# Expert stages of a two-layer diffusion backbone: ScalarE splits a tile ahead of weighing a gathered pick, and layer two's last V chunk moves to the U tiles' PSUM bank

## The reference, cut to what matters

```python
def peer(h, w_q, sub_keys, u_tab, v_tab):
    experts, gates = peer_route(hf, w_q, sub_keys)     # 8 heads x 16 picks of 16384 experts, per token
    def block(args):
        hb, eb, gb = args
        a = jnp.einsum('td,tkd->tk', hb, u_tab[eb])
        w = gb.astype(hb.dtype) * jax.nn.gelu(a, approximate=False)
        return jnp.einsum('tk,tkd->td', w, v_tab[eb])
...
    x = x + mod[5] * peer(modulate(rmsnorm(x, ln2_w[layer]), mod[3], mod[4]),
                          p_w_q[layer], p_sub_keys[layer], p_u[layer], p_v[layer])
```

## Time and profile before

| what | value |
|---|---|
| median of 3 runs | 4219.02 us (4217.18 to 4225.48) |
| profiled execution, span | 4219.0 us |
| its own time beside the span | 4219.0 us on the same clock: nothing lies around the span |
| PE busy | 3869.5 us (92%) |
| DVE busy | 3528.4 us (84%) |
| ACT busy | 1945.1 us (46%) |
| POOL busy | 1105.8 us (26%) |
| mean HBM traffic | 241 GB/s over the span |
| Gelus of layer one (L1939), first to last start | 1078.3 to 2396.7 us |
| Gelus of layer two (L1939), first to last start | 3236.0 to 4184.3 us |

### The profile page before, as it was taken

How to read it: one execution, slowest core, us unless ns; L and a number is a source line. 1 busy time by engine, 2 the same in 40 slices (tenths; PEclk the granted TensorE clock), 3 DMA queues, 4 the chain that set the end, 5 groups by cost and what they waited for, 6 DMA issues and landing times. The chain is left out here.

```text
span 4219.0 us, 69815 instructions
## 1 busy us (share of the span) xinstructions
PE 3869.5 (92%) x23631; PEld 3337.2 (79%) x23631; DVE 3528.4 (84%) x6910; ACT 1945.1 (46%) x3599; POOL 1105.8 (26%) x1095
## 2 busy tenths in 40 slices
PE   7969989988999999999999897898868999999998
PEld 6854468877888888888888776336767999999998
DVE  5387948999799999999999966666998899999998
ACT  4367532147444444444444355654246444444443
POOL 0000000039443434434334300000046333333332
PEclk9979999869999999999999998999979999999999
DMA  5102321246899999999999821112237999999997
GB/s 194 55 17 65 89 67 46 70 123 191 326 382 364 381 364 381 370 372 370 384 366 383 333 66 46 44 45 77 68 100 247 371 369 376 369 376 369 377 368 290
DMA packets 246997, 1018.18 MB, mean 241 GB/s; under 512 B 17121, under 2 KB 115521, under 8 KB 146641
## 3 DMA queue, kind: packets, MB, share of 16 engines
q0 software_dynamic: 85296, 599.59, 36.7%
q1 hardware_dynamic: 161504, 416.31, 28.2%
HBM read 963.34 MB, written 52.43 MB: 241 GB/s over the span
## 5 line engine op out<-in xcount | busy, mean ns | idle before, releaser
L1397 POOL DMA_INDIRECT rows<-rows,pick_i x512 | 790.6, 1544 | 1156.5 <-DVE y_tok L2663 653.2
L525 PE MATMUL psA<-h_hi,split_hi 128*128 128x448 f32 (+3 forms) x2768 | 971.8, 351 | 88.8 <-DVE xT L2642 54.7
L2027 DVE TENSOR_TENSOR split_lo<-raw,split_hi 128x1024 fp32r<-128x1024 f32 x596 | 727.9, 1221 | 303.2 <-ACT split_hi L1441 296.8
L525 PE MATMUL psA<-h_lo,split_hi 128*128 128x448 f32 (+3 forms) x2768 | 952.1, 344 | 0.0
L525 PE MATMUL psA<-h_hi,split_lo 128*128 128x448 f32 (+3 forms) x2768 | 951.8, 344 | 0.0
L1441 ACT ACTIVATE split_hi<-raw 128x1024 fp32r<-128x1024 f32 x596 | 628.3, 1054 | 304.2 <-DMA raw<-expert_pairs 153.4
L525 PEld LDWEIGHTS psA<-h_hi,split_hi 128*128 128x128 f32 x2768 | 527.5, 191 | 165.6 <-issue 112.8
L2651 DVE CUSTOM_DVE_ANT_1 rows<-rows,h_wide 128x1024 f32<-128x1024 f32 x512 | 624.8, 1220 | 25.5 <-DMA rows<-rows,pick_i 23.4
L2663 DVE SCALAR_TENSOR_TENSOR y_tok<-rows,pick_w,y_tok 128x1024 f32<-128x1024 f32 x444 | 569.1, 1282 | 5.9
L525 PEld LDWEIGHTS psA<-h_hi,split_lo 128*128 128x128 f32 x2768 | 527.3, 190 | 35.6
L525 PEld LDWEIGHTS psA<-h_lo,split_hi 128*128 128x128 f32 x2768 | 527.9, 191 | 33.3
(11 more groups left out here) (344 smaller groups left out, 6321.3 us busy)
## 6 DMA issues: line engine op xcount, KB each, us to landing
raw<-expert_pairs SPq DMA_DIRECT2D x256, 1024.0 KB, 7.2
gates<-g_buf SPq DMA_DIRECT2D x22, 2048.0 KB, 8.7
raw<-tiles SPq DMA_DIRECT2D x84, 512.0 KB, 3.7
raw<-mod_tiles SPq DMA_DIRECT2D x80, 512.0 KB, 3.6
g_in<-gates POOLq DMA_DIRECT2D x32, 896.0 KB, 9.0
g_in<-gates POOLq DMA_DIRECT2D x32, 640.0 KB, 5.9
mod_w<-mod_pairs SPq DMA_DIRECT2D x8, 1024.0 KB, 19.9
rows<-rows,pick_i POOLq DMA_INDIRECT x512, 8.4
```

Source lines behind the costliest of these rows:

```text
L525: ins = nc.tensor.matmul(out_, lhsT, rhs, start=start, stop=stop)
L1397: nc.gpsimd.indirect_dma_start(rows[l][:, b, :], None, (rows0, rows1)[l], bass.IndirectOffsetOnAxis(pick_i[:, u:u + 1], 0))\
L2027: V.tensor_tensor(split_lo[:, n % SPLIT].rearrange("p k n -> p (k n)"), raw[:, n % RAW, :], split_hi[:, n % SPLIT].rearrange("p k n -> p ( ...
```

## The change

Two edits. ScalarE's order around the second Gelu becomes Gelu of u1, split base+2, weigh (before: Gelu, weigh, split); the picks weighed per superblock and their order stay. And layer two's eighth V chunk is treated as layer one's: no longer two resident pieces, but one chunk of 320 columns formed in `psA[0]` after the second Gelu and added to `xT` by VectorE once per superblock. With `CYCLED[1]` no longer None, these lines of before run in layer two as well: TensorE waits for `cycled_free` ahead of u0, `tile_passed` of v0 is given after the cycled chunk instead of after v0's own chunks, VectorE waits for `cycled_full` and adds.

```diff
-RESIDENT = (tuple((k, 0, DENSE[0][1], k, 0) for k in range(KD - 1)),
-            tuple((k, 0, DENSE[1][1], k, 0) for k in range(KD - 1)) +
-            ((KD - 1, 0, 192, 0, 320), (KD - 1, 192, 320, 1, 320)))
-CYCLED = (KD - 1, None)
+RESIDENT = tuple(tuple((k, 0, DENSE[l][1], k, 0) for k in range(KD - 1)) for l in range(DEPTH))
+CYCLED = (KD - 1, KD - 1)
 DRAIN = ((0, 2, 4), (1, 3), (5, 6))
@@ scalar engine, experts(l)
                 for c in range(2):
                     if s + 1 < NSUPER:
                         gelu(c, s + 1)
-                    weigh(spread[2 * c])
+                    if c == 0:
+                        weigh(spread[0])
                     split_to(min(base + c + 1, end))
-                    weigh(spread[1] if c == 0 else 0)
+                    weigh(spread[1 + c])
```

## The result

The changed kernel takes 4110.4 us (median of 4, 4106.6 to 4111.6) against 4218.4 us before: ratio 0.974, 95% interval 0.972 to 0.975. It is faster, by 108 us.

The account below looks back on a forecast made before the run. VectorE's loop, with its idle behind ScalarE's split, was taken to set the pace of both expert stages. 4219.0 less 44 (layer one) less 38 (layer two) gave 4137, stated as 4138 us; range 4115 to 4182.

Parts of the forecast that it names:

- ScalarE's order, VectorE's idle: Both layers: splitting before weighing removes VectorE's whole idle, 1.08 us per superblock in layer one and 1.21 in layer two.
- What is late next in layer one: Layer one: TensorE and VectorE become level at about 19.7 us per superblock, gaining at most 58 us.
- The transfers of layer one: Layer one: 7.80 MB per superblock at 391 GB/s gives a 19.95 us floor; superblock taken as 19.9, gain 44 us.
- Layer two: Layer two: cycled chunk and new order bring the superblock from 14.98 to 14.35 us, within 14.2 to 14.5; gain 38 us.
- (d): Layer two: ScalarE's existing wait for the U pair's transfer costs nothing yet; its window grows by 0.5 us.
- (a): Layer two: TensorE's next U tile must wait for VectorE's add, a short wait of 0.1 to 0.2 us per superblock.
- (b): Layer two: the cycled chunk must wait for the second Gelu, which is done two us before.
- (c): Layer two: first V tile's slot returns only after the cycled chunk; ScalarE's split still fits with 0.1 us to spare.
- the transfers as bound: Rival: transfers bound layer one, superblock 20.25 us, gain 24; layer two at 14.5 gains 29; 4166 us; chance 0.19.
- the ring's late slot: Rival: returned slot or add late by 0.8 us keeps layer two at 14.98 us; 4175 us in all; chance 0.13.
- the slower one: Rival: TensorE waits over 1.5 us for layer two's add; at 16.0 us a superblock, 4237 us; chance 0.05.
- the order that does nothing: Rival: ScalarE's split waits for its transfer or slot anyway, so the time stays 4219 us; chance 0.03.

Follow-up runs that it names:

- the extra load: Changed kernel plus a 0.459 MB HBM load into unused SBUF, all 128 partitions, in each of 60 layer-one superblocks; 4142.7 us.
- part 1 alone: Kernel of before with only ScalarE's split moved ahead of the weighing, both layers, layer two's resident pieces kept; 4123.0 us, ratio 0.977.

## Why the prediction was wrong, and where it was right

*ScalarE's order, VectorE's idle:* right. Both idles went whole, as the two timelines show, and the order alone is worth 94 us. The prediction itself had 44 + 26 = 70 for it (26 from 14.98 to 14.55 in 61 superblocks of layer two); the 99 expected ahead of that run were set with the result known.

*What is late next in layer one:* right in kind, TensorE and VectorE level. The size was read too coarsely: I bracketed TensorE's loop at 19.63 to 19.89 us and then took 19.7 as the fastest that could be; it is 19.63, and it is TensorE's own, which hardly waits any more.

*The transfers of layer one:* this is the step that failed. I made a floor, 7.80 MB / 391 GB/s = 19.95 us, out of a window whose share was 1.00, and set the superblock to 19.9. The changed kernel runs at 7.80 / 19.63 = 397 GB/s; its gathers were late less often than before, where I had expected more. A share near 1.00 was not the engines' limit: they gave 409 in the mean when asked, and 421 over whole superblocks. Nor was the window one superblock of 19.7 us. By its Gelus (1323.83 to 1344.00) that superblock took 20.17 us, and VectorE waited in it 1.08 us for `split_hi` and never for gathered rows: the 391 GB/s were what was asked for. The trace of before had a superblock faster than my floor, which I did not look for (TensorE catching up behind a long one); from Gelu to Gelu:

```profile
1534.22:1553.86 19.64, 19.64 (x97) 18.05 (x96) 18.51 (x24) 8.65 (x19) 8.99 (x6) 1.00 1.01 405
```

This term, 0.27 us in some 60 superblocks, is 16 us of the 28 that I missed.

*The number of superblocks:* I multiplied the regular superblock of 20.65 by 61. The stage had longer ones too: the mean from the fourth on was 20.88 before and is 19.71 now. Those of 21.6 to 23.8 us stood behind late gathers and, five times, with a fall of TensorE's clock; most are gone. That is some 9 us, and the 2 us taken off for more late gathers were wrong in sign. The first three superblocks gave 2 us more. Together 72.6 where I had 44. The clock itself played no part: from the add at 1296.64 to the next at 1317.29, across the fall at 1299, VectorE took its regular 20.65 us, and so or nearly so at the other four (20.65, 20.66 and 20.66; 21.08 with a gather 0.87 us late).

*The limit of HBM that the Trainium skill states* (DMA: Bandwidth & Descriptors, "Where 436 GB/s comes from"), 358 GB/s, is passed by the changed kernel over 850 us by a wider margin, 397 GB/s, and by 409 with the extra load.

*Layer two:* the number was right, its working in part. Superblock 14.37 us against 14.35, 36 us of stage against 38. VectorE's loop with the add was put at 14.21 and TensorE's at 14.1 to 14.2; the short superblocks take 14.13. But what lifted 14.2 to 14.35 was a floor of 14.3 us made of 389 GB/s, the same reading as in layer one; the long superblock from 3582.63 to 3597.39 ran at 411 GB/s. What lengthens the long ones is (d), the U pair, for which I had counted a wider window and no longer landing, and put the cost at nothing. That the mean of short and long ones meets 14.35 is partly luck. Of (a), TensorE's wait for the add, 6.9 us are 0.12 a superblock, as forecast; without the gate loads it is 0.5 us in all, so it too came from the late pair. (b) and (c) did not show as a wait of their own. The add costs 0.46 where I took 0.44. That part 1 alone would give about 14.55 here was measured as 14.53.

*The rivals:* the transfers as bound, the ring's late slot, the slower one and the order that does nothing did not come about. That the cycled chunk alone would be slower than before, I had not said.

## What to carry to other kernels

Where an engine idles behind a second engine which itself waits for the first, look for a closed loop: here the idle was part of the period and hid nothing, and reordering two instructions on the idle-looking engine was worth seven times as much as 0.4 us less of matmuls per superblock. A transfer rate seen at a steady state can be no more than the demand of that state; before taking it for a ceiling, look for a stretch in which something waits for transfers, or add traffic and see where the period moves, superblock by superblock, as a mean can hide that only every second one is hit. And multiply by the mean period of a stage (last minus first start), not by its commonest one.

## What the runs showed of the hardware that I had not expected

- The DMA share does not rank states: it was 1.00 to 1.01 at 384, at 405 and at 409 GB/s, and 1.01 again over a superblock at 421.
- A load of 0.229 MB per superblock into 64 partitions brought the rate of all traffic down to 384 GB/s; the same bytes into 128 partitions left it at 405 (one run each). The full load, with the same 3.6 KB a partition but into all 128, ran at 409, so the size of the pieces is not the reason. What is was not tested.
- Six small matmuls of 192 and 128 columns took about as long as four of 320 (0.62 us against 4 x 0.147 = 0.59), and replacing them was worth 14.53 - 14.13 = 0.40 us a superblock where nothing else waited.
